# Two blocks of a transformer on one core: the layers of a block in one program, memory projections first, index columns first

## The reference

```python
# block one, layer l
h = rmsnorm(x, g_mix[l])
dq, dk, dv, c_q, c_kv_kr, xq, gate_logits = split(h @ w_in[l])
y_diff = diff_attention(...) @ w_diff_o[l]        # causal, 8 heads, two softmax maps each
y_mla  = latent_attention(...) @ w_mla_o[l]       # causal, 8 heads, low-rank q and kv
mem_n  = rmsnorm(mem, mem_gain[l])                # mem: 256 x 1024, the same for both layers
kv     = mem_n @ w_mem_kv[l]                      # "mk" and "mv": keys and values of the memory
y_mem  = cross_attention(xq, kv) @ w_cross_o[l]
x = x + (gates[0]*y_diff + gates[1]*y_mla + gates[2]*y_mem) @ w_out[l]
x = x + square(relu(rmsnorm(x, g_mlp[l]) @ w_mlp1[l])) @ w_mlp2[l]

# block two, layer l
z = rmsnorm(x, norm_w_2[l]) @ w_in_2[l]
# a: attention over the 128 keys of each row with the highest index score,
#    score = sum over 8 index heads of relu(q_idx . k_idx) * weight
# b: attention in three kinds (compressed, selected, window); c: convolution; d: pooling
x = x + concat(a, b, c, d) @ w_out_2[l]
```

## Time and profile before

| what | value |
|---|---|
| median of 3 runs | 2855.99 us (2854.02 to 2857.33) |
| the profiled execution, its own time | 2849.83 us |
| its span, first to last instruction | 2847.3 us |
| TensorE busy | 2639.5 us, 93% of the span |
| GpSimd busy | 1878.1 us, 66% |
| VectorE busy | 1105.7 us, 39% |
| ScalarE busy | 781.9 us, 27% |
| mean granted clock of TensorE | 0.965 of full speed |

### The profile page before, as it was taken

One profiled execution on the slowest core, in us unless ns is written; L12 is line 12 of the kernel. 1 busy time (PEld: TensorE's weight loads), 2 busy tenths in 40 slices (PEclk: granted clock), 3 DMA queues, 4 the chain that ended last, 5 costly groups with the idle time before them and its releaser, 6 DMA issues. The chain is left out here.

```text
span 2847.3 us, 37707 instructions
## 1 busy us (share of the span) xinstructions
PE 2639.5 (93%) x13724; PEld 2125.6 (75%) x13724; DVE 1105.7 (39%) x1836; ACT 781.9 (27%) x1581; POOL 1878.1 (66%) x1562
## 2 busy tenths in 40 slices
PE   6999889999999997999889999999998997979897
PEld 5788567877888886778667778888887975678655
DVE  4454655111210113444575210310102398526983
ACT  3332474000120202342375100120111233313261
POOL 4747514888898995847621888898896872367604
PEclk9999899999999998999999999999998997999989
DMA  4322101233223222322200233223223430043202
GB/s 121 104 58 80 41 9 38 89 93 93 93 96 97 93 98 78 115 70 66 65 9 16 82 93 97 88 96 96 96 97 77 105 84 27 32 86 89 74 1 74
DMA packets 159284, 214.74 MB, mean 75 GB/s; under 512 B 51696, under 2 KB 69360, under 8 KB 159088
## 3 DMA queue, kind: packets, MB, share of 16 engines
q1 hardware_dynamic: 120336, 207.27, 23.9%
q10 hardware_dynamic: 38752, 4.95, 1.4%
HBM read 210.06 MB, written 2.10 MB: 75 GB/s over the span
## 5 line engine op out<-in xcount | busy, mean ns | idle before, releaser
L293 POOL TENSOR_TENSOR weight_parts<-weight_ring,zero 128x512 fp32r<-128x512 f32 (+3 forms) x736 | 796.2, 1082 | 741.4 <-PE ps L376 365.4
L296 POOL TENSOR_TENSOR weight_parts<-weight_ring,weight_parts 128x512 fp32r<-128x512 f32 (+3 forms) x804 | 1063.8, 1324 | 129.1 <-ACT weight_parts L304 70.9
L378 PE MATMUL ps<-h_feature_major_high,weight_parts 128*128 128x512 f32 x2304 | 589.5, 394 | 12.2 <-POOL weight_parts L293 11.6
L378 PEld LDWEIGHTS ps<-h_feature_major_high,weight_parts 128*128 128x128 f32 x2304 | 427.6, 188 | 119.7 <-POOL weight_parts L293 19.3
L376 PE MATMUL ps<-weight_parts,h_feature_major_high 128*128 128x512 f32 (+3 forms) x1920 | 437.4, 366 | 20.7 <-POOL weight_parts L293 8.9
L376 PEld LDWEIGHTS ps<-weight_parts,h_feature_major_high 128*128 128x128 f32 x1920 | 338.3, 190 | 75.5 <-POOL weight_parts L293 10.3
L378 PE MATMUL ps<-h_feature_major_low,weight_parts 128*128 128x512 f32 x1152 | 309.6, 391 | 0.0
L376 PE MATMUL ps<-weight_parts,ut_high 128*128 128x512 f32 x1024 | 254.7, 390 | 0.0
L378 PEld LDWEIGHTS ps<-h_feature_major_low,weight_parts 128*128 128x128 f32 x1152 | 217.3, 189 | 46.3
L524 PE MATMUL ps<-arena 64*128 64x512 f32 (+9 forms) x704 | 176.3, 502 | 74.3 <-ACT probs L641 56.4
L376 PE MATMUL ps<-weight_parts,h_feature_major_low 128*128 128x512 f32 (+3 forms) x960 | 230.6, 362 | 0.0
(11 more groups left out here) (264 smaller groups left out, 2911.3 us busy)
## 6 DMA issues: line engine op xcount, KB each, us to landing
weight_ring<-in_w_in SPq DMA_DIRECT2D x272, 256.0 KB, 2.6
weight_ring<-in_w_mlp SPq DMA_DIRECT2D x256, 256.0 KB, 2.6
weight_ring<-in_w_out SPq DMA_DIRECT2D x64, 256.0 KB, 2.6
weight_ring<-in_w_mem_kv SPq DMA_DIRECT2D x32, 256.0 KB, 2.6
weight_ring<-in_w_diff_o SPq DMA_DIRECT2D x32, 256.0 KB, 2.7
weight_ring<-in_w_in SPq DMA_DIRECT2D x32, 170.0 KB, 2.6
weight_ring<-in_w_in SPq DMA_DIRECT2D x32, 168.0 KB, 2.2
weight_ring<-in_w_in SPq DMA_DIRECT2D x32, 163.0 KB, 2.2
```

The costliest lines, as they stand in the source:

```text
L293: self.nc.gpsimd.tensor_tensor(high, raw, self.m["zero"][:].broadcast_to([P, raw.shape[1]]), ALU.add).then_inc(self.s["slab_high"], 1)
L296: self.nc.gpsimd.tensor_tensor(low, raw, high.bitcast(F32), ALU.subtract).then_inc(self.s["slab_split"], 1)
L378: last = self.nc.tensor.matmul(banks[:, t, :], w[:, cut], h, **ends)
```

## The change

- **Layers in one program.** The hardware loops go. `run_layers` builds both layers of a block, each with its own semaphores, and each engine runs through one layer's stream and then the next one's without a barrier. A new layer's first slabs wait for the slots and buffers of the previous layer's last (`last_before`, `wait_used`), its first groups for that layer's banks. Between the blocks a clear and a barrier remain.
- **Memory first.** `mk` and `mv` stand at the head of a layer of block one, ahead of `xq`. They share one half of the banks (`beside`), the transposes of `x` are woven in ahead of `mk`'s slab 7 and `mv`'s slab 5, and ScalarE writes the high part of 13 of their 16 slabs (before: 9), taking turns with the pieces of `x`. For the first layer `mem` is loaded and squared in the prologue, ahead of half of `x`. For the second it is loaded, normed and transposed inside the MLP of the first (`next_mem_t`, ahead of slab 10 of `down00`). The vectors of a layer other than the first one or two are loaded behind `mv`.
- **Last slab by tile.** In `wo1` of both blocks and in `down11`, the last slab is multiplied tile by tile (`last_slab_by_tile`), and `add_right` waits for each tile.
- **Norm of a layer of block one.** VectorE scales three of four tiles and ScalarE the last, instead of two each.
- **Index columns first.** Block two projects `za1` before `za0`. Index columns are rotated and transposed alone (`i_t`, inside `zb0`); scores of i = 1 are inside `zb0`, of i = 2 inside `zb1`, of i = 3 inside `f0`. `choose(1)` comes ahead of the rotation of the b columns, `choose(2)` right behind it.
- The clearing of `pool_w` moves from GpSimd to VectorE.

```diff
-        with nc.Fori(0, DEPTH) as layer:
-            block_one(nc, io, m, one, layer)
-            nc.gpsimd.sem_clear(layer_sems)
-            nc.all_engine_barrier()
-        with nc.Fori(0, DEPTH) as layer:
-            block_two(nc, io, m, one, layer)
-            nc.gpsimd.sem_clear(layer_sems)
-            nc.all_engine_barrier()
+        run_layers(nc, block_one, io, m, signals)
+        nc.gpsimd.sem_clear(layer_sems)
+        nc.all_engine_barrier()
+        run_layers(nc, block_two, io, m, signals)
...
+            elif self.prev:
+                sp.wait_ge(self.prev.s["slab_split"], self.last_before(n, SLOTS) + 1)
...
+            sp.dma_start(view(m["probs"][:].rearrange("p a b n -> p (a b n)"), 0, 2, D),
+                         io["mem"].rearrange("a (t p) d -> p (a t) d", p=P)).then_inc(mem_landed, 16)
             for t in range(2, TT):
                 sp.dma_start(m["x"][:, t, :], io["x"][0, t * P:(t + 1) * P, :]).then_inc(x_landed, 16)
...
+    def last_slab_by_tile(self, pe, g, n, k, banks, act):
+
+        pe.wait_ge(self.s["slab_split"], n + 1)
+        for t in range(TT):
+            for i, (a, b) in enumerate(((0, 0), (1, 0), (0, 1))):
+                w, h = self.m["parts"][:, n % PARTS, b, 0:W512], act[a][:, g.get("at", 0) + k, t * P:(t + 1) * P]
+                last = self.nc.tensor.matmul(banks[:, t, 0:W512], h, w, start=False, stop=i == 2)
+            if t < TT - 1:
+                last.then_inc(self.s["tile_full"], 1)
+        return last
...
-            L.turn_rows(pe, ("h_t0", "h_t1"), hn, (("h_normed", 1), ("h_normed_act", 1), ("h_normed", 2), ("h_normed_act", 2)))
-            pe.wait_ge(s["mem_normed"], 1)
-            L.turn(pe, "mem_t", [(c // 2, (c % 2) * MEM + t * P, memx[:, t, c * P:(c + 1) * P]) for c in range(KC) for t in range(2)])
+            if layer:
+                prev.emptied(pe, "next_mem_t")
+            else:
+                turn_mem("mem_t")
+                L.emptied(pe, "mem_t")
+            L.project(pe, "mk", memt, {7: lambda: turn_h(0)})
+            L.project(pe, "mv", memt, {5: lambda: turn_h(1)})
             L.project(pe, "xq", ht, when_emptied("h_t0", "h_t1"))
-            L.emptied(pe, "mem_t")
-            L.project(pe, "mk", memt)
-            L.project(pe, "mv", memt)
             L.project(pe, "dq0", ht)
...
+            L.norm_last(act, st_h, x, hn)
+            act.wait_ge(s["small_loaded"], n_first * 16)
...
+            L.write_slab_highs(act, range(mk0 + 3, mv0))
+            for k in range(4):
+                L.write_slab_highs(act, [mv0 + k])
+                high_of("h_t0", [k])
...
-            L.project(pe, "zb1", ht, {3: lambda: turn_a(0), 6: lambda: turn_a(1)})
-            L.project(pe, "ag", ht, {2: first_index, 4: lambda: index_scores(1, 1)})
-            L.project(pe, "f0", ht, {1: lambda: turn_b(0), 3: lambda: turn_b(1), 5: lambda: index_scores(2, 0), 7: lambda: index_scores(2, 1)})
-            L.project(pe, "bg", ht, {2: lambda: index_scores(3, 0), 6: lambda: index_scores(3, 1)})
+            L.project(pe, "zb0", ht, {2: turn_index, 5: first_index, 7: lambda: index_scores(1, 1)})
+            L.project(pe, "zb1", ht, {2: turn_a, 4: lambda: index_scores(2, 0), 6: lambda: index_scores(2, 1)})
+            L.project(pe, "ag", ht)
+            L.project(pe, "f0", ht, {0: lambda: turn_b(0), 2: lambda: turn_b(1), 5: lambda: index_scores(3, 0), 7: lambda: index_scores(3, 1)})
+            L.project(pe, "bg", ht)
```

More of the change, by code:

```diff
@@ L74, in __init__ @@
         self.names = list(groups)
-        hosts = [n for n in self.names if "inside" not in groups[n]]
+        hosts = [n for n in self.names if "inside" not in groups[n] and "beside" not in groups[n]]
         self.half = {n: k % 2 for k, n in enumerate(hosts)}
+        self.half |= {n: self.half[groups[n]["beside"]] for n in self.names if "beside" in groups[n]}
         self.half |= {n: 1 - self.half[groups[n]["inside"]] for n in self.names if n not in self.half}
@@ L316, in begin @@
         half = self.order.half[name]
-        if self.last[half]:
-            self.emptied(pe, self.last[half])
+        if "beside" not in self.groups[name]:
+            if self.last[half]:
+                self.emptied(pe, self.last[half])
+            elif self.prev:
+                self.prev.emptied(pe, self.prev.last[half])
         self.last[half] = name
@@ L698, in block_one @@
     groups = {
-        "h_t0": parts, "h_t1": parts, "mem_t": parts,
+        **({} if layer else {"mem_t": dict(parts, inside="mk")}),
+        "h_t0": dict(parts, inside="mk"), "mk": tok(io["w_mem_kv"], 0, W512, tiles=2),
+        "h_t1": dict(parts, inside="mv"),
+        "mv": tok(io["w_mem_kv"], W512, W512, tiles=2, beside="mk"),
         "xq": tok(w_in, C_XQ, W512),
-        "mk": tok(io["w_mem_kv"], 0, W512, tiles=2), "mv": tok(io["w_mem_kv"], W512, W512, tiles=2),
         "dq0": tok(w_in, 0, W512, by="dve"), "xq_t": dict(turned, inside="dq1"), "mk_t": dict(turned, inside="dq1"),
@@ L835, in block_one @@
     ]
-    n_small = 16 * len(small)
+    n_small, n_first = 16 * len(small), 1 if layer else 2
     def four(name, dst, at, gains, width=SEQ):
@@ L1110, in _ @@
             for f in range(2):
+                if layer == 0 and f == 1:
+                    roots(st_mem)
+                    act.wait_ge(s["next_gain_loaded"], 16)
+                    L.write_high("next_mem_t", split["next_mem_t"])
                 for j in range(ups):
                     k = f * ups + j
+                    if layer == k == 0:
+                        with nc.allow_non_contiguous_dma("gains of the next layer, four bytes each"):
+                            act.dma_start(*mem_gain(1)).then_inc(s["next_gain_loaded"], 16)
                     full(act, f"up{f}{j}")
@@ L1395, in _, with block_two @@
             L.add_right(dve, "down11", 2, st_h)
-def block_two(nc, io, m, s, layer):
+    return block
+def block_two(nc, io, m, s, layer, prev):
     w_in, x, ht, arena, outs, ps, ident = io["w_in_2"], m["x"], m["ht"], m["arena"], m["outs"], m["ps"], m["ident"]
@@ L1489, in block_two @@
               for j in range(4)] for k in range(2)]
-    with nc.Block() as block:
+    block = Programs(L)
+    if True:
         @block.sync
```

337 lines of the change are left out of this document (227 added, 110 removed).

## The result

The changed kernel takes 2823.9 us (median of 4 executions, 2820.3 to 2828.8) against 2855.5 for the kernel before in the same rounds (2854.0 to 2857.3): the ratio is 0.9894, 95% interval 0.988 to 0.991. That is 31.5 us less, where 42.2 were forecast. The profiled execution is the longest of the four: 2828.8 us, span 2827.0, against 2849.8 and 2847.3 before. From trace to trace only 20.3 us of the span are gone, 22 fewer than forecast, and half of what follows is about these. One execution of e11 took 5254.8 us where the kernel's others took 2846.7 to 2859.8, and is left out of all comparisons.

A forecast was written before the change was run, and what follows sets the result against it. TensorE's work and waits bound the kernel (busy 93%). Gains 26.5 + 5.9 + 3.8 + 1 + 5 = 42.2 us off 2849.8 gave 2807.6, with 6.2 added back 2813.8, said as 2814; range 2803 to 2828.

The forecast's parts named there:

- the memory stage: Sign in block one: the memory's projections with the transposes woven in take 28 to 30 us; the sum used 28.9.
- the wait in `f0`: Sign in both layers of block two: TensorE waits on VectorE for 6 to 9 us; the sum used 7.9.
- attention not earlier than 176 to 180 us: Sign of being wrong, block two: attention begins no earlier than that after the layer's first projection.
- Between block one's layers: From the end of `down11` to `dq0`: gain of 28.5 us, less transposes of `mem` in `down00`, net 26.5.
- rival 2: Second layer of block one: `g_mix` lands late, slab 3's high part comes 5.5 us later; 2820 us, chance 0.12.
- The transposes in `down00`: 16 transposes of `mem` cost 1.7 us plus 0.3 for restarting; their norm and splitting lie hidden under `down00`.
- Between block two's layers: VectorE's norm step comes 1.6 us after the last matmul instead of 7.65, less 0.15: 5.9 us gained.
- By tile: Last slab by tile before a barrier, at the ends of block one and block two: 1.9 us gained each.
- The start: Loading `mem` ahead of half of `x` costs 3.8 us, yet `dq0` comes at 84.9 instead of 85.9: 1 us gained.
- Index columns first: Block two: choosing earlier brings attention forward, 2.5 us gained in each layer, 5 together; bounds 0 and 5 per layer.
- attention 48.2 later: Block two, VectorE's chain: distance in us from the compression's rotation to attention, taken from the trace before.
- Rival 1: Block two: b columns cost more than the index gains, attention begins 2 to 3 us later; 2824 us, chance 0.15.

The follow-up runs named there:

- e11: The kernel before, unchanged, run again for a second trace: 2854.9 us.
- e5: e4 with the memory's second sums of squares left away: 2819.4 us against 2820.9.
- e2: The kernel before with only block two's new order, index columns first: 2860.1 us against 2853.8, ratio 1.0016.
- e9: The changed kernel with the last slab of `wo1` and `down11` over all tiles at once again: 2831.1 us.
- e1: The changed kernel with block two back in its old order, all else changed: 2822.7 us.
- e0: The changed kernel run again, unchanged: 2823.5 us, ratio 0.9886.
- e4: e3 with the steps of VectorE's convolution handed out one by one inside attention: 2820.9 us.
- e8: e3 without the memory's second squares, b columns' transposes in slabs 4 and 6 of `f0`, compression's steps inside `choose(2)` and `choose(3)`: 2804.2 us, ratio 0.983.
- e3: The changed kernel with the b columns' transposes at slabs 3 and 5 of `f0`, scores of i = 3 back in `bg`: 2813.7 us.

## Why the prediction was right, and where it was not

The sign, and the range, were right because the bulk of the gain lies at the boundaries, and those were priced from rows of the same waits. In size it was 11 to 12 us too high: the forecast proper, 2808 to 2819, was missed, and only the wider range holds the result. Of its marks, `down11` to `mk`, the clock there, the wait at attention, the 13 us between block two's layers and `mk` at 32.5 came; the memory stage took 30.6 where 28 to 30 stood, the wait in `f0` 5.6 and 5.3 where 6 to 9 stood. One of the marks for wrong came too: attention not earlier than 176 to 180 us. By its own steps:

- **Between block one's layers** (26.5 net): measured 26.9 less 3.6, so 23.3. The memory stage of 28.9 took 30.6; 0.85 of the difference is the wait for `mk` and `mv` to be emptied (1.45, taken as 0.6). The gain of the load (`g_mix`) was no trouble, so rival 2 fell. The transposes in `down00` were priced at 2.0 and cost 3.6: "they would cost only if they were over 20 us late" looked at the operands' date, not at what VectorE's passes do to GpSimd, whose parts TensorE waits for in that stage (1.4 us, e5).
- **Between block two's layers** 5.9: measured 6.0 against the trace of the prediction, 7.5 and 8.0 against the 42.5 and 43.0 us of e2 and e11. The term is right for its own trace; that it hit to 0.1 is luck. **By tile** 1.9 twice: 2.8 and 2.4 in the trace, and e9, which takes that edit alone back, has 1.8 at both.
- **The start** 1, with `dq0` at 84.9: it came at 84.2 and 86.1 in two traces, 85.9 and 84.4 (e11) before. The load of the memory cost 2.4 us, not 3.8 (and the terms for `mk`'s start add up to 33.15, not 33.3). That the start gained anything is not shown.
- **Index columns first** 5: this step failed. e1 and e0 differ by 0.8 us, and e2 has the order 6.3 us slower by itself. The stall was there and a little shorter than forecast (5.6 against 7.9), and the rotation of the compression came where I put it (129.5 us after the first projection, forecast 128.6). From there I wrote "attention 48.2 later", a distance copied from a trace in which GpSimd was idle at its end. Moved 6 us forward, the same VectorE instructions lay beside GpSimd's splitting: 51.3. I had counted GpSimd's idleness as a gain (1.4) where TensorE stands, and not its work as a loss where VectorE had been alone. Rival 1 has the right outcome (attention not earlier, near 2824) with another cause than the one it named: the time is where it said by coincidence, since the order accounts for only 5.8 of its 10 us.
- **TensorE's clock in attention.** No term. The profiled execution before had one stretch at the lower level per layer and was 4 to 6 us shorter than the medians; I added the difference back as a constant, though it is part of what is compared. Attention takes 82.8 / 82.8 and 82.8 / 85.5 in the two traces of the kernel before, and 89.4 / 88.6 and 86.2 / 88.6 in those of the changed one. On the mean of the four that is 4.8 us a layer. Part is chance (e11). What makes the rest is open: e1 has it with the old order (87.6 / 85.4), e2 with the old layering (89.2 / 87.4).

Counted on the medians, of the 12 us missing the order accounts for 5.8 (e0 against e1, 0.8 instead of -5.0, each median good to some 2 us) and the memory's transposes for 1.6. The stage between block one's layers is 1.6 short, and the two last boundaries brought 1.4 more than their terms. What is left, some 4 us, is of the size of the clock's changes.

## What to carry to other kernels

When a chain on VectorE is moved in time, don't carry its length along: look at what GpSimd does at the new place, for every instruction of the chain to its end, and in the other direction at what VectorE's new passes do to GpSimd if TensorE lives on it. A wait that shrinks is no gain: read the distance from a fixed point ahead to the one behind the wait (here first projection to attention, 179.9 and 180.7, or 179.5 and 178.7 in the second layer). And where a stage hovers between two clocks, take a second trace of the kernel before ahead of pricing anything under 1%.

## What the runs showed of the hardware

- The same four scalar_tensor_tensor of 128x512 on VectorE took 2.90 us with GpSimd idle, 6.19 beside its splitting, 2.82 handed out in attention (e4). GpSimd's own 1.04 us copy took 2.02 beside VectorE's squares. The reduction of 128x3072 took 5.70 to 5.71 us with GpSimd busy for 4.7 us of it (before), 3.7 (after) or 2.5 (e8).
- A stage of small matmuls in which TensorE is busy over 90% ran between 82.8 and 89.4 us with the same instructions, 70.8 to 72.1 us (73.7 once) plus half of the 22 to 36 us at the lower level. In all ten layers of the profiled run after, e0, e1, e2 and e3 the clock fell again 10 to 21 us after it had risen, in the four layers of the kernel before once. Ahead of such a fall TensorE had been busy 8.28 of 10.20 us at the full clock (the second window above); in the trace before it was busy 54.3 of 58.9 us and no fall came.
- A barrier of all engines, with the weights' loads behind it, cost 6.9 to 7.1 us where TensorE then lives on the first slab, and 2.4 to 2.5 where a norm comes first; the medians of the two runs (2822.2 and 2826.7 against 2823.5) did not show it.
